# The overflow loop of a mixture of experts moved ahead of the last expert, whose rows are added by 0/1 products, and three of eight final tiles scaled by two other engines

## The reference, cut to what matters

```
h2 = rms_norm(x, norm2_g) * (1 + sc2) + sh2
# gates: for each token two of the 32 experts
hg = einsum('nd,edf->nef', hf, w_gate);  hu = einsum('nd,edf->nef', hf, w_up)
act = silu(hg) * hu * gates
x = x + gt2 * einsum('nef,efd->nd', act, w_down)
return x * rsqrt(mean(x * x) + eps) * final_g
```

## Time and profile before

| | us |
|---|---|
| median of 3 runs | 873.32 (872.92 to 874.47) |
| the profiled execution: its time | 874.96 |
| the profiled execution: its span, first to last instruction | 873.2 |

### The profile page before, as it was taken

The page is one execution under the profiler, slowest core; times in us unless marked ns, Lnnn a source line. Parts: engine busy times, 40 slices in busy tenths (PEclk is TensorE's granted clock), DMA queues, the critical chain, the costliest instruction groups (busy, mean ns, idle before and its releaser), DMA issues. The chain is left out here.

```text
span 873.2 us, 17369 instructions
## 1 busy us (share of the span) xinstructions
PE 815.8 (93%) x7175; PEld 544.7 (62%) x7175; DVE 460.3 (53%) x1154; ACT 240.4 (28%) x581; POOL 278.8 (32%) x267
## 2 busy tenths in 40 slices
PE   8999999999999999799888999999999999999950
PEld 8557544544444355777777455555788888888830
DVE  3750478887830136467664244434645555454534
ACT  6220111112200143455543112221233223232214
POOL 5810000000499501452741100000135565543332
PEclk9999999999999999999999999999999999999995
DMA  9934433445111123000000881112889989888639
GB/s 315 324 90 135 145 120 121 139 158 172 37 38 36 27 70 133 18 3 4 4 4 20 308 325 48 49 73 96 325 296 301 303 285 273 277 267 261 206 73 367
DMA packets 79719, 136.35 MB, mean 156 GB/s; under 512 B 17213, under 2 KB 51226, under 8 KB 79642
## 3 DMA queue, kind: packets, MB, share of 16 engines
q1 hardware_dynamic: 69338, 118.44, 39.0%
q0 software_dynamic: 10304, 16.82, 8.2%
HBM read 124.18 MB, written 29.92 MB: 176 GB/s over the span
## 5 line engine op out<-in xcount | busy, mean ns | idle before, releaser
L792 PE MATMUL banks<-REG_W 128*128 128x512 f32 (+2 forms) x832 | 274.6, 499 | 0.9 <-DVE pend L1988 0.5
L792 PEld LDWEIGHTS banks<-REG_W 128*128 128x128 f32 (+1 forms) x832 | 125.9, 182 | 135.3 <-issue 133.8
L792 PE MATMUL banks<-REG_W,REG_Y 128*128 128x512 f32 x256 | 118.3, 599 | 1.4 <-DVE REG_Y L2236 1.1
L1434 ACT ACTIVATE REG_P<-banks 128x256 f32<-128x256 f32 (+2 forms) x126 | 53.5, 463 | 156.8 <-PE banks L792 137.7
L792 PE MATMUL banks<-REG_P 64*64 64x64 f32 (+3 forms) x2752 | 79.5, 230 | 13.1 <-issue 8.9
L792 PEld LDWEIGHTS banks<-REG_P 64*64 64x64 f32 (+1 forms) x2752 | 67.6, 135 | 23.0 <-issue 16.4
L1434 ACT ACTIVATE REG_Y<-banks,mod,s 128x128 f32<-128x128 f32 x136 | 51.2, 457 | 85.8 <-PE banks L1386 85.8
L792 PEld LDWEIGHTS banks<-REG_W,REG_Y 128*128 128x128 f32 x256 | 45.6, 191 | 44.3 <-issue 44.2
L792 PEld LDWEIGHTS banks<-REG_Y,REG_P 128*128 128x128 f32 (+1 forms) x616 | 63.1, 181 | 7.0 <-issue 7.0
L792 PE MATMUL banks<-REG_Y,REG_P 128*128 128x128 f32 (+1 forms) x616 | 66.6, 276 | 0.1
L636 POOL TENSOR_TENSOR REG_P<-REG_P 128x1040 f32<-128x1040 f32 x2 | 4.8, 2390 | 175.8 <-DVE REG_P L1801 175.8
(11 more groups left out here) (295 smaller groups left out, 1108.1 us busy)
## 6 DMA issues: line engine op xcount, KB each, us to landing
REG_P<-in_w_ada SPq DMA_DIRECT2D x20, 1024.0 KB, 6.2
REG_W<-in_w_in SPq DMA_DIRECT2D x17, 512.0 KB
REG_P<-in_moe_w_gate SPq DMA_DIRECT2D x17, 512.0 KB, 8.3
REG_W<-in_moe_w_gate SPq DMA_DIRECT2D x16, 512.0 KB, 6.4
REG_W<-in_moe_w_up SPq DMA_DIRECT2D x16, 512.0 KB, 10.7
REG_W<-in_moe_w_down SPq DMA_DIRECT2D x16, 512.0 KB, 16.7
REG_P<-in_moe_w_up SPq DMA_DIRECT2D x14, 512.0 KB, 14.9
REG_P<-in_moe_w_down SPq DMA_DIRECT2D x12, 512.0 KB, 21.2
```

Of the source, the lines that this page charges most:

```text
L792: return pe.matmul(o_, l, r, start=start, stop=stop, skip_group_check=True)
L1434: return act.activation(o_, i_, f, **kw)
```

## The change

- **Order.** The overflow loop runs ahead of expert 31 (`LAST`) on all engines. TensorE's order is now: transposes of overflow tile 0, down of expert 30, the loop, then gate, up and down of expert 31. In the loop the transposes of the next tile stand ahead of the down product. GpSimd gathers the second overflow tile ahead of the scatter of expert 30.
- **Expert 31's rows** are not scattered into `y_d`. Its result stays in `yo`, and VectorE builds for each of the eight token tiles a 0/1 matrix `hot[:, j]` (row of the expert against token of the tile). TensorE multiplies `hot[:, j]` with the result, two products of 512 columns for each tile, and VectorE adds the product from PSUM to the loaded tile (`completed(j)`). SyncE loads `y_d` when the loop's last `ov_go` is raised. A gather buffer is zeroed once, before the experts, since every lane of expert 31 is now read.
- **Tail.** Tiles 1, 3 and 5 (`HELPED`) are scaled by the root on ScalarE in place and multiplied by final_g on GpSimd, and no longer by VectorE.

```diff
+        hot, _ = area(REG_W, SLOT, NT, P)
+        LAST = E - 1
+        HELPED = (1, 3, 5)
@@ sync
-            sp.wait_ge(s["f_go"], 1)
+            sp.wait_ge(s["ov_go"], n_ov + 1)
 
             for j in range(NT):
                 sp.dma_start(x1[:, j], y_d[j * P:(j + 1) * P, :]).then_inc(s_w[j], 16)
             for j in range(NT):
-                sp.wait_ge(s["f_o"], j + 1)
+                if j in HELPED:
+                    sp.wait_ge(s["f_og"], HELPED.index(j) + 1)
+                else:
+                    sp.wait_ge(s["f_o"], j + 1 - len([g for g in HELPED if g < j]))
@@ gpsimd
-            for e in range(2, BUF):
-                gather(TURN[e], e)
+            gather(TURN[2], 2)
+            ch.step(gp.memset(xg[3], 0.0))
+            gather(TURN[3], 3)
...
-            for e in range(E):
+            for e in range(LAST):
+                if e == LAST - 1:
+                    gp.wait_ge(s["m_tx"], E + 1)
+                    gather(E + 1, 0)
                 gp.wait_ge(s["m_yd"], e + 1)
                 scatter_add(rows_of(TURN[e], 0), e % RES)
                 gather_behind(e + 3)
-                if e == E - 1:
-                    gp.wait_ge(s["m_tx"], E + 1)
-                    gather(E + 1, 0)
...
             with gp.Fori(0, n_ov) as i:
                 ch.enter(i, 4)
-                scatter_add(rows_of(i + E, 1, i + (E + 1)), 0)
+                scatter_add(rows_of(i + E, 1, i + E), 2)
...
-            gp.sem_inc(s["f_go"], 1)
-
+
+            gp.wait_ge(s["xr_ld"], 16 * (NT + 1))
             for i in range(NT // 2):
                 gp.wait_ge(s["f_ss"], i + 1)
                 at = slice(2 * i, 2 * i + 2)
                 gp.tensor_tensor(rs[:, 2, at], ss[:, 2, at], mhalf[:, 0:2], ALU.pow).then_inc(s["rstd_ready"], 1)
+                if i >= 1:
+                    j = HELPED[i - 1]
+                    gp.wait_ge(s["op_xn"], NT + i)
+                    gp.tensor_tensor(x1[:, j], x1[:, j], fg, ALU.mult).then_inc(s["f_og"], 1)
@@ tensor
-            for e in range(1, E):
-                if e + 1 < E:
-                    ex_t(e + 1, (e + 1) % BUF, 16 * ((e + 1) // BUF + 1))
+            for e in range(1, LAST):
+                ex_t(e + 1, (e + 1) % BUF, 16 * ((e + 1) // BUF + 1))
...
             ex_t(E, 0, 16 * (E // BUF + 1))
-            ex_dn(E - 1, (E - 1) % 2, (E - 1) % RING)
+            ex_dn(LAST - 1, 0, (LAST - 1) % RING)
...
             with pe.Fori(0, n_ov) as i:
                 ex_gu(i + E, 0, 0, "m_", s["ov_w"], i * 48 + 48, False)
-                pe.wait_ge(s["m_yd"], i + E)
-                ex_dn(i + E, 0, 0, "m_", False)
                 ex_t(i + (E + 1), 0, i * 16 + 16 * (E // BUF + 2))
+                pe.wait_ge(s["m_yd"], i + LAST)
+                ex_dn(i + LAST, 0, 0, "m_", False)
+
+            ex_gu(LAST, 1, LAST % RING, wsem=s_w[LAST % RING], wcount=w_loads(LAST % RING, LAST // RING + 1), wait_free=False)
+            ex_dn(n_ov + LAST, 1, LAST % RING, wait_free=False)
+            beside(8, 2)
+            for j in range(NT):
+                q = 2 * ((j + 1) % 4)
+                if j == 3:
+                    pe.wait_ge(s["m_xa"], n_ov + (E + 1))
+                    pe.wait_ge(s["m_xd"], n_ov + (E + 1))
+                if j >= 4:
+                    pe.wait_ge(s["op_x1"], NT + j - 3)
+                for h in range(2):
+                    if j == 0:
+                        pe.wait_ge(s["m_yd"], n_ov + (E + h))
+                    last = mm(PS[q + h][:, :], hot[:, j, :], yo[LAST % RES][:, h * 512:(h + 1) * 512])
+                last.then_inc(s["op_ps"], 1)
@@ scalar
+            hidden(n_ov + LAST, 1, free=False)
             for j in range(NT):
-                act.wait_ge(s_w[j], w_loads(j, len(range(j, E, RING))) + 16)
+                act.wait_ge(s["op_x1"], NT + j + 1)
...
                 fn(fsq[:, j % 2], x1[:, j], ACT.Square, scale=ROOT, accum_out=ss[:, 2, j:j + 1]).then_inc(s["ss_ready"], 1)
+                if j - 2 in HELPED:
+                    act.wait_ge(s["rstd_ready"], 2 * NT + (j - 2) // 2 + 1)
+                    fn(x1[:, j - 2], x1[:, j - 2], scale=rs[:, 2, j - 2:j - 1]).then_inc(s["op_xn"], 1)
@@ vector
-            result(E - 1, (E - 1) % 2)
+            result(LAST - 1, 0)
+
+            ch.step(dve.tensor_copy(gap[:, 0:1], tbl[:, TURN[LAST], 0:1]))
+            ch.step(stt(left[:, :], i32[:, 0:NT], -float(P), gap[:, 0:1].to_broadcast([P, NT]), ALU.mult, ALU.add))
+            for j in range(NT):
+                ts(hot[:, j, :].rearrange("p (a b) -> p a b", a=KD), i128[:, :].rearrange("p (b a) -> p a b", a=KD), left[:, j:j + 1], None, ALU.is_equal)
...
+            def completed(j):
+                dve.wait_ge(s_w[j], w_loads(j, len(range(j, E, RING))) + 16)
+                dve.wait_ge(s["op_ps"], NT + j + 1)
+                q = 2 * ((j + 1) % 4)
+                tt(x1[:, j], x1[:, j], banks[:, q:q + 2, :].rearrange("p a d -> p (a d)"), ALU.add).then_inc(s["op_x1"], 1)
+
+            completed(0)
+            completed(1)
+            completed(2)
...
-            root_args(0)
             for i in range(NT // 2):
-                if i + 1 < NT // 2:
-                    root_args(i + 1)
+                root_args(i)
+                if 2 * i + 3 < NT:
+                    completed(2 * i + 3)
                 dve.wait_ge(s["rstd_ready"], 2 * NT + i + 1)
                 for j in (2 * i, 2 * i + 1):
-                    stt(x1[:, j], x1[:, j], rs[:, 2, j:j + 1], fg, ALU.mult, ALU.mult).then_inc(s["f_o"], 1)
+                    if j not in HELPED:
+                        stt(x1[:, j], x1[:, j], rs[:, 2, j:j + 1], fg, ALU.mult, ALU.mult).then_inc(s["f_o"], 1)
+                    if j == 2 * i and 2 * i + 4 < NT:
+                        completed(2 * i + 4)
```

More of the change, by code:

```diff
@@ L263, in build @@
         fsq, _ = area(REG_W, 0, 2, D)
+        hot, _ = area(REG_W, SLOT, NT, P)
+        LAST = E - 1
+        HELPED = (1, 3, 5)
+        assert LAST % RING == 9 and LAST % RES == 1
         ident = sb("ident", [P, P])
@@ L771, in _ @@
             for b in range(RES):
[L772 removed]
+                gp.wait_ge(s_sc[b], 16 * len(range(b, LAST, RES)))
             with gp.Fori(0, n_ov) as i:
                 ch.enter(i, 4)
[L775 removed]
+                scatter_add(rows_of(i + E, 1, i + E), 2)
                 gp.wait_ge(s_gx[0], i * 16 + 16 * (E // BUF + 2))
@@ L778, in _ @@
                 fetch(at, 0)
-                gp.wait_ge(s_sc[0], i * 16 + 16 * (len(range(0, E, RES)) + 1))
+                gp.wait_ge(s_sc[2], i * 16 + 16 * (len(range(2, LAST, RES)) + 1))
                 gp.sem_inc(s["ov_go"], 1)
-            gp.sem_inc(s["f_go"], 1)
+            gp.wait_ge(s["xr_ld"], 16 * (NT + 1))
             for i in range(NT // 2):
@@ L1672, in _ @@
             modulated(xt[:, 0], 0, 1, "m_tx", "m_xa", 0)
-            for e in range(E):
-                if e + 1 < E:
-                    modulated(xt[:, (e + 1) % 2], 0, e + 2, "m_tx", "m_xa", 0)
+            for e in range(LAST):
+                modulated(xt[:, (e + 1) % 2], 0, e + 2, "m_tx", "m_xa", 0)
                 hidden(e, e % 2, free=e >= 2)
@@ L1680, in _ @@
             with act.Fori(0, n_ov) as i:
-                hidden(i + E, 0, free=False)
+                hidden(i + LAST, 0, free=False)
                 modulated(xt[:, 0], 0, i + (E + 2), "m_tx", "m_xa", 0)
+            hidden(n_ov + LAST, 1, free=False)
             for j in range(NT):
-                act.wait_ge(s_w[j], w_loads(j, len(range(j, E, RING))) + 16)
+                act.wait_ge(s["op_x1"], NT + j + 1)
                 if j >= 2:
@@ L2236, in hidden, with scaled_halves @@
                 stt(ac[:, par, :], a1[:, par, :], 0.5, PS[2 + par][:, P:2 * P], ALU.mult, ALU.mult).then_inc(s[pre + "act"], 1)
+            def scaled_halves(b, par, by):
+                return [stt(yo[b][:, h * 512:(h + 1) * 512], PS[4 + 2 * par + h][:, :], by, gtb[:, 1, h * 512:(h + 1) * 512],
+                            ALU.mult, ALU.mult) for h in range(2)]
             def result(e, par, pre="m_"):
-                b = e % RES if isinstance(e, int) else 0
+                b = e % RES
                 dve.wait_ge(s[pre + "dn"], e + 1)
-                if isinstance(e, int) and e >= RES:
+                if e >= RES:
                     dve.wait_ge(s_sc[b], 16 * (e // RES))
-                for h in range(2):
-                    last = stt(yo[b][:, h * 512:(h + 1) * 512], PS[4 + 2 * par + h][:, :], gate(TURN[e] if isinstance(e, int) else e), gtb[:, 1, h * 512:(h + 1) * 512],
-                               ALU.mult, ALU.mult)
-                last.then_inc(s[pre + "yd"], 1)
+                scaled_halves(b, par, gate(TURN[e]))[1].then_inc(s[pre + "yd"], 1)
             modulated(xt[:, 0], 1, "m_tx", "m_xd", 1)
-            for e in range(E):
-                if e + 1 < E:
-                    modulated(xt[:, (e + 1) % 2], e + 2, "m_tx", "m_xd", 1)
+            for e in range(LAST):
```

(16 more changed lines are left out.)

2 lines of the change are left out of this document (1 added, 1 removed).

## The result

| | before | after |
|---|---|---|
| median, us | 873.12 (870.51 to 874.47, 4 executions) | 882.12 (880.29 to 883.45, 4 executions) |
| profiled execution: its time, its span, us | 874.96, 873.2 | 881.25, 879.5 |

The ratio is 1.0107, 95% interval 1.008 to 1.0135: slower, by 9.0 us at the medians. The forecast was 883.0 (876.0 to 886.5).

A forecast was written before the change was run, and what follows sets the result against it. TensorE was taken to set the pace up to 826 us, different limits after. Last scaling 877.2 + 1.7 (clock) = 878.9 against 868.9, 10.0 more; with 4.0 instead of 4.3 behind it, 9.7 more: 883.0, range 876.0 to 886.5.

The forecast's parts named there:

- the overflow comes no earlier: Overflow loop's start: gather and weights hold it as before, so TensorE has nothing to do for 5.6 us.
- The rival in which it starts early: Overflow loop: gather and weights land with TensorE's arrival, gate matmuls 5.8 us earlier, 869.1 us in all; chance 0.05.
- the clock falls: TensorE before the overflow's transposes: 5.6 us idle drops the granted clock to half, costing 1.7 us on the path.
- the rival that it holds: TensorE's idle stretch: the clock stays up until the gather lands, giving 881.3 us; chance 0.15.
- the first 3.4 us of work run at half speed: TensorE from the overflow's transposes on: half clock for 3.4 us of matmuls, so 1.7 us lost.
- the start of the loads: First reload of y_d: 1.7 us later by the clock, 0.5 earlier by SyncE's wait, so +1.2 us.
- the gate matmuls not before 834.80: Overflow tile's gate matmuls on TensorE: start can't precede 834.80 us, where it was before the change.
- The rival in which they hide under the reload: Tail: products and additions all hide under the y_d loads, 872.4 us, no change that can be told; chance 0.04.
- the port: Tail: VectorE scalings with both inputs in SBUF wait for GpSimd's multiplications, losing 2.0 and 2.1 us; last pair shares it.
- no port wait: Tail: GpSimd's multiplications leave VectorE alone, giving 876.6 us; chance 0.10.
- My order: Predicted instruction sequence of the tail, from additions at 852.4 us to the last scaling at 877.2, without clock loss.
- what lies behind the last scaling: End of the span: the last store, 4.0 us behind the last scaling instead of 4.3.

The follow-up runs named there:

- e9: Kernel after without helped tiles, 0/1 products and additions, so expert 31's rows are missing in the output; ratio 1.0018, 874.09 us.
- e12: Kernel after without helped tiles and without the sixteen 0/1 products; the eight additions stay and add what the banks hold; ratio 1.0086, 879.9 us.
- e1: Kernel after with no tile given to ScalarE and GpSimd, VectorE scaling all eight; ratio 1.0088, 879.67 us.
- e5: Kernel after with VectorE's scalings reading final_g from a PSUM copy, products rotating over three pairs of banks instead of four; ratio 1.0078, 878.9 us.
- e8: Kernel after without helped tiles and with expert 31 back ahead of the overflow loop, its rows still added by products; ratio 1.0056, 876.86 us.
- e2: Kernel after with 24 filler matmuls on TensorE ahead of the wait for the overflow tile's gather; ratio 1.0094, 880.23 us.
- e3: Kernel before with only tiles 1, 3 and 5 scaled by ScalarE and multiplied by GpSimd; ratio 1.0065, 878.23 us.
- e4: Kernel after with 24 filler matmuls ahead of the gather wait and VectorE scaling all eight tiles; ratio 1.0056, 876.24 us.
- e10: Kernel before with one more one-column GpSimd multiplication that waits for all eight VectorE scalings; ratio 1.0058, 875.33 us.
- e6: Kernel before with one more GpSimd wait, for the load of final_g, ahead of its powers; ratio 0.9992.
- e11: Kernel before with SyncE's wait ahead of the y_d loads put on the last increment inside the overflow loop; ratio 0.9995.
- e7: Kernel before with tiles 1, 3 and 5 on ScalarE and GpSimd, and VectorE's scalings reading final_g from PSUM; ratio 1.0027, 874.44 us.

## Why the prediction was right, step by step

**Right: the overflow comes no earlier, and TensorE idles.** Idle 5.64 us (said: 5.6), gather 8.25 us (8.2). The rival in which it starts early is refuted: the gate matmuls stand at +15.29, before at +13.08.

**Right that the clock falls, wrong for how long.** It fell 4.2 us into the idle time (4.1 in the earlier trace rows), and the rival that it holds is refuted. The step that failed is "the first 3.4 us of work run at half speed": the half clock lasted 6.83 us here, in e9 and in e12, and 3.41 only in e1 and e5. The price is the time from the overflow's transposes to its gate matmuls: 5.17 us here and 5.18 in e9 and e12, 4.06 in e1, and 2.84 in e8, where the clock stays up. So 3.4 us of half clock cost 1.2 and not 1.7, and the 6.8 of this execution cost 2.3, or 2.1 against the 3.05 of the kernel before. That is within my bounds (0 to 3.4), and near the 1.7 only because the two errors go against each other. Where it lasted 6.8 us the clock had fallen 3.9 to 4.3 us into the idle time, where 3.4, 4.8 to 4.9; what decides it no run tells. "TensorE: Matmul & The Clock Gate" of the Trainium skill, section "HAM oscillation — how this bites in real kernels", describes this wait for a DMA with cold matmuls behind it; the trace agrees.

**Off: the start of the loads.** I had +1.2 (1.7 less 0.5) and it was +2.0: the gather landed 0.1 later, from the transposes to the gate matmuls it was 2.1 more, and from there to the first load only 0.2 less (14.06 instead of 14.28). I also took "the gate matmuls not before 834.80" as a fixed time. It is the landing of the overflow weights, and this moves between executions, from +10.8 in e1 to +14.7 in e5. In the kernel after it costs nothing, as e9 shows, since the half clock holds the gate matmuls longer; in e2, e3, e4 and e5 the weights are the last wait.

**Right: 0/1 tiles, memset, the second gather, expert 31 behind the loop cost nothing.** The tiles were 0.19 us away from costing something. The first product at 848.85 is the 850.3 + 1.7 of the forecast less the 3.2 between the executions, to 0.1 us.

**Right: products 1.72 us a tile (1.74), additions 1.2 (1.22).** What VectorE's load made of it is as the sum had it: 5.1 us of the tail are additions (e12 against e9), and no more than 0.3 are products. The rival in which they hide under the reload is refuted by e9, with 5.4 us less.

**Right: the port.** Two scalings at 3.15 and 3.13, each ending behind a GpSimd multiplication of 2.36, and the last pair serialized. The rival "no port wait" is refuted by the rows and priced by e5, 4.9 us of tail. With e1 the balance is plain: three tiles moved save VectorE 3.4 us and the lock takes 4.9.

**Off: the length of the tail.** My order gave 877.2 - 848.6 = 28.6 from the first load to the last scaling; it was 26.76. The order was right to the instruction; the terms were each a little long: the first addition 3.3 us behind the first load instead of 3.8 (it waited for that load, where I had it wait for the first product, and 850.3 and 1.72 make 852.0 for that and not 852.2), consecutive VectorE instructions that start 1.13 to 1.20 apart though each lasts 1.21 to 1.28, and a wait of 1.9 instead of 2.0 and 2.1 at the port.

**Wrong: what lies behind the last scaling.** I let the last store set the end and took 4.0 instead of 4.3. The store did land sooner (2.95 us behind instead of 3.90), but the end came 4.84 behind, because GpSimd's last multiplication ended at 872.36 and the drain behind it at 879.24. The model of the end was wrong, by 0.8 us.

**The sum.** 9.7 forecast, 9.5 in the profile, 9.0 at the medians. Three errors stand in it: +0.8 for the start of the loads, -1.8 for the tail, +0.8 behind it. They cancel to 0.2. The port, the additions and the fall of the clock were right; the length of the half clock and what sets the end were not, and the closeness of the number is partly luck.

## What to carry to other kernels

Before an engine is relieved, look at what bounds the stretch: here the reload and the stores filled the DMA engines in the tail, so VectorE's slack was free, and additions of 9.7 us used it up and 5 more. Work handed to GpSimd while VectorE runs SBUF-only operations can cost more than it saves; one operand in PSUM on VectorE's side took nearly the whole loss in the tail away (4.9 us, e5). Work that fills a wait for a DMA, as expert 31 did, isn't free to move: the gap that it leaves costs the clock as well. And where sums are compared with one execution, mark both traces at a common event first.

## What the hardware showed that I had not expected

**GpSimd's closing drain.** In all fourteen profiles it ends 6.88 to 6.96 us behind GpSimd's last instruction (before: 865.83 to 872.79; after: 872.36 to 879.24; e1: 870.25 to 877.12; e10: 862.69 to 869.63), and the span ends 0.2 to 0.4 us behind the later of this and the landing of the last store. Before, and in e6 and e11, both fall together (before: 872.79 and 872.76). After, and in the others, the drain is the later one; by e10 it is shown to set the end, in the rest it is read off the same two marks. VectorE's own drain ends 0.06 us behind its last instruction (868.92 and 868.86, before). In e7 and e5, whose GpSimd multiplications are not held up and whose VectorE ends early, it is why a tail as short as before, or 4.9 us shorter than after, ends late all the same.

**The landing of the overflow weights** spread from +10.8 to +14.7 between executions of kernels that issue them at the same place; what spreads it I have not found.
